# Sums by token for the convolution's norm, and half of the first residual turned ahead of the last output block

## The reference

```python
def conformer_conv(u, lw):
    a, b = jnp.split(u, 2, axis=-1)
    g = a * jax.nn.sigmoid(b)
    g = lax.conv_general_dilated(g, lw['conv_dw'][:, None, :], ...)     # 31 taps, by channel
    g = layernorm(g + lw['conv_b'], lw['conv_ln_g'], lw['conv_ln_b'])   # over the 1024 channels
    return jax.nn.silu(g) @ lw['w_conv_o']

# token_mixer:
merged = jax.nn.sigmoid(ga) * y_att + jax.nn.sigmoid(gc) * y_conv
return merged @ lw['w_out']

# first_block:
xs = xs + g1 * token_mixer(hx, lw, rope, k_c, v_c)
hx = modulate(rmsnorm(xs, norm2_g[l]), sh2, sc2)
xs = xs + g2 * peer_ffn(hx, lw)                                        # begins with hx @ peer_wq
```

## Time and profile before

| | |
|---|---|
| median of 3 runs | 2242.8 us (2241.54 to 2243.55) |
| the profiled execution | 2253.25 us, of which the span is 2251.4 us |
| TensorE busy | 95% of the span, mean granted clock 0.981 |
| VectorE, ScalarE, GpSimd busy | 76%, 42%, 41% |
| the norm (from the channel sums to the first product with `w_co`) | 468.0 to 495.5 us |
| the first residual (from the last product with `w_out` to the first with `peer_wq`) | 593.0 to 615.2 us |

### The profile page before, as it was taken

One profiled execution on the slowest core, in us unless ns is written; L12 is line 12 of the kernel. 1 busy time (PEld: TensorE's weight loads), 2 busy tenths in 40 slices (PEclk: granted clock), 3 DMA queues, 4 the chain that ended last, 5 costly groups with the idle time before them and its releaser, 6 DMA issues. The chain is left out here.

```text
span 2251.4 us, 29546 instructions
## 1 busy us (share of the span) xinstructions
PE 2136.3 (95%) x10685; PEld 1831.2 (81%) x10685; DVE 1705.4 (76%) x3336; ACT 937.5 (42%) x1480; POOL 929.4 (41%) x614
## 2 busy tenths in 40 slices
PE   6998999989799999799889999999999999999998
PEld 3886787767688999799878888888888888777767
DVE  5886989886634999999678888878888897744243
ACT  3445555443333344344333333333333343445472
POOL 0251222100453655599634454434555551542222
PEclk9999999999999999899999999999999999999999
DMA  7322021345362554455889999998999994321111
GB/s 301 103 91 78 33 94 57 126 150 196 132 198 78 168 163 156 132 202 225 297 323 368 342 356 358 363 347 318 375 349 361 359 359 158 108 84 47 48 47 47
DMA packets 177136, 455.84 MB, mean 202 GB/s; under 512 B 13792, under 2 KB 80736, under 8 KB 175328
## 3 DMA queue, kind: packets, MB, share of 16 engines
q1 hardware_dynamic: 136912, 293.57, 38.2%
q0 software_dynamic: 36864, 134.23, 15.9%
q10 hardware_dynamic: 3216, 26.15, 3.1%
HBM read 409.86 MB, written 44.04 MB: 202 GB/s over the span
## 5 line engine op out<-in xcount | busy, mean ns | idle before, releaser
L1757 POOL TENSOR_TENSOR Rl<-raw,Rh 128x1024 fp32r<-128x1024 f32 x156 | 401.5, 2580 | 846.7 <-ACT Rh L1258 846.2
L1258 ACT ACTIVATE Rh<-raw 128x1024 fp32r<-128x1024 f32 x380 | 399.9, 1056 | 340.6 <-DMA raw<-in_u 105.6
L723 PE MATMUL bank<-XAh,Rh 128*128 128x384 f32 (+1 forms) x1280 | 458.7, 358 | 9.4 <-ACT gt L1592 4.2
L725 PE MATMUL bank<-XAh,Rl 128*128 128x384 f32 (+1 forms) x1280 | 444.9, 348 | 0.0
L724 PE MATMUL bank<-XAl,Rh 128*128 128x384 f32 (+1 forms) x1280 | 444.7, 347 | 0.0
L1793 POOL DMA_INDIRECT ga<-in_v,eid x128 | 197.5, 1543 | 185.9 <-DVE y L2433 158.4
L1841 DVE TENSOR_TENSOR Rl<-raw,Rh 128x1024 fp32r<-128x1024 f32 x212 | 260.4, 1230 | 7.3 <-ACT Rh L1258 7.2
L1793 POOL DMA_INDIRECT ga<-in_un,eid x128 | 172.7, 1349 | 221.1 <-DVE act L2425 183.6
L723 PEld LDWEIGHTS bank<-XAh,Rh 128*128 128x128 f32 x1280 | 243.0, 190 | 21.2 <-issue 6.9
L724 PEld LDWEIGHTS bank<-XAl,Rh 128*128 128x128 f32 x1280 | 242.9, 190 | 10.8
L725 PEld LDWEIGHTS bank<-XAh,Rl 128*128 128x128 f32 x1280 | 242.2, 189 | 10.5
(11 more groups left out here) (335 smaller groups left out, 4019.5 us busy)
## 6 DMA issues: line engine op xcount, KB each, us to landing
raw<-in_u SPq DMA_DIRECT2D x128, 512.0 KB
raw<-in_v SPq DMA_DIRECT2D x128, 512.0 KB
wd<-wb ACTq DMA_DIRECT2D x12, 2048.0 KB, 7.2
wg<-wd SPq DMA_DIRECT2D x30, 768.0 KB
raw<-in_w_mod SPq DMA_DIRECT2D x32, 512.0 KB
raw<-in_w_in SPq DMA_DIRECT2D x32, 512.0 KB
gd<-pk SPq DMA_DIRECT2D x64, 192.0 KB, 1.9
gt<-gd SPq DMA_DIRECT2D x16, 768.0 KB, 11.3
```

The lines of the kernel that those rows point to most:

```text
L723: e.matmul(o, sh, mh, start=first, stop=False)
L725: return e.matmul(o, sl, mh, start=False, stop=last)
L1258: e.activation(Rh[:, r % NRING, :], raw[:, n % NRAW, :], ACT.Copy).then_inc(s["hi"], 1)
L1757: e.tensor_tensor(Rl[:, r % NRING, :], raw[:, n % NRAW, :], Rh[:, r % NRING, :].bitcast(F32), ALU.subtract).then_inc(s["lo"], 1)
```

## The change

**The norm.** The matrix that adds the channels up for the mean is now `mean8`, filled once with 1/1024, so that the result in PSUM is the mean, and the eight subtractions read it there. The squares are summed by token: each 128 x 128 piece of a block of squares is the stationary operand and one column of ones the moving one, so that the result is 128 tokens by 4 (column `tb`). Variance, root and reciprocal are then taken on 128 x 4 elements. Four diagonal matrices (`dgr`: the identity, each row scaled by its token's reciprocal) times the all-ones matrix spread the result over all partitions, in PSUM (`rsd`), and the eight multiplications read it there. TensorE does this ahead of ao 7. On VectorE `merge_att(5)` moves behind the norm, to 6 and 7.

**The residual.** After wo 6 TensorE turns the four halves with i = 0 (blocks 0 to 3 of `cout`), then does wo 7, and then the four with i = 1. VectorE adds the first four, with `mod_bias`, and adds an epsilon to their sums of squares, all between the evictions of wo 6 and wo 7. ScalarE squares 128 x 512 at a time. The order of the root, the reciprocal and the normed block over the four token blocks is staggered: the mean square of block b + 1 stands ahead of `h2` of block b.

```diff
+    use(("rsd",), 4, 0)
     for cb in range(8):
+        if cb == 7:
+            for tb in range(4):
+                use(("x1", tb, 0), 4 + tb)
         use(("wo", cb), cb % 4)
     for tb in range(4):
-        for i in range(2):
-            use(("x1", tb, i), 4 + (2 * tb + i) % 4)
+        use(("x1", tb, 1), 4 + tb)
...
             for cb in range(8):
                 e.wait_ge(s["conv"], cb + 1)
-                t = e.matmul(o[:, :], ones[:, :], cout[:, cb, :], start=(cb == 0), stop=(cb == 7))
+                t = e.matmul(o[:, :], mean8[:, :], cout[:, cb, :], start=(cb == 0), stop=(cb == 7))
...
                 e.wait_ge(s["sqc"], cb + 1)
-                e.matmul(o[:, :], ones[:, :], lt[cb % 4][:, :], start=(cb == 0), stop=(cb == 7)).then_inc(s["ltv"], 1)
+                for tb in range(4):
+                    t = e.matmul(o[:, tb:tb + 1], lt[cb % 4][:, tb * 128:(tb + 1) * 128], ones[:, 0:1],
+                                 start=(cb == 0 and tb == 0), stop=(cb == 7 and tb == 3))
+                t.then_inc(s["ltv"], 1)
+            o, done = hold(("rsd",))
+            e.wait_ge(s["sub"], 8)
+            for tb in range(4):
+                e.wait_ge(s["dgr"], tb + 1)
+                t = e.matmul(o[:, tb * 128:(tb + 1) * 128], ones[:, :], dgr[:, tb, :], start=True, stop=True)
+            t.then_inc(done, 1)
             merge_att(7)
...
+            def turned_out(i):
+                for tb in range(4):
+                    o, done = hold(("x1", tb, i))
+                    if tb == 0:
+                        u = USES["wo", 4 * i + 3]
+                        e.wait_ge(free[u.bank], u.done)
+                    for k in range(4):
+                        t = e.transpose(o[:, k * 128:(k + 1) * 128],
+                                        cout[:, 4 * i + k, tb * 128:(tb + 1) * 128], ident[:, :])
+                    t.then_inc(done, 1)
             for cb in range(8):
+                if cb == 7:
+                    turned_out(0)
                 gemm_T(("w_o", cb), XB, ("wo", cb), merged_ready if cb == 0 else None)
-            add_T("x1", lambda k, sl: cout[:, k, sl], y1_ready)
+            turned_out(1)
... ScalarE
-            for b in range(4):
-                u = USES["x1", b, 1]
-                e.wait_ge(free[u.bank], u.done)
-                e.activation(jk2[:, :], x1[:, b, :], ACT.Square, accum_out=sml[:, 128 + 2 * b:129 + 2 * b]
-                             ).then_inc(s["sqd"], 1)
-                root(f"h2{b}", sml[:, 129 + 2 * b:130 + 2 * b])
+            for i in range(2):
+                for b in range(4):
+                    u = USES["x1", b, i]
+                    e.wait_ge(free[u.bank], u.done)
+                    o = 104 + 4 * i + b
+                    e.activation(jk2[:, 0:512], x1[:, b, 512 * i:512 * i + 512], ACT.Square, accum_out=sml[:, o:o + 1]
+                                 ).then_inc(s["sqd"], 1)
+                    if i:
+                        root(f"h2{b}", sml[:, 112 + b:113 + b])
... VectorE
-            e.tensor_scalar(mu[:, :], bank[u.bank][:, :], 1.0 / D, None, ALU.mult).then_inc(free[u.bank], 1)
             for cb in range(8):
-                e.tensor_tensor(cout[:, cb, :], cout[:, cb, :], mu[:, :], ALU.subtract).then_inc(s["sub"], 1)
+                e.tensor_tensor(cout[:, cb, :], cout[:, cb, :], bank[u.bank][:, :], ALU.subtract).then_inc(s["sub"], 1)
...
+                if cb == 6:
+                    e.wait_ge(s["x1"], 16)
+                    added(0)
+                    t_mod = mod_bias(24, 40, 0, n_own)
+                    e.wait_ge(s["sqd"], 4)
+                    t_sq = own(e.tensor_scalar(sml[:, 104:108], sml[:, 104:108], D * EPS, None, ALU.add))
+            added(1)
```

More of the change, by code:

```diff
@@ L452, in build @@
         lu = [at(f"lu{i}", FB + 60 + 2 * i, [128, 512]) for i in range(4)]
-        mu = at("mu", FB + 64, [128, 512])
-        rsd = at("rsd", FB, [128, 512])
+        mean8 = at("mean8", 70, [128, 128])
+        dgr = at("dgr", FB, [128, 4, 128])
         x1 = at("x1", FB + 44, [128, 4, 1024])
@@ L942, in merged_ready @@
                 e.wait_ge(s["mRl"], k + 1)
+            def turned_out(i):
[4 more added lines that the diff above has]
+                        e.wait_ge(free[u.bank], u.done)
+                    e.wait_ge(s["cn"], 8)
+                    for k in range(4):
+                        t = e.transpose(o[:, k * 128:(k + 1) * 128],
+                                        cout[:, 4 * i + k, tb * 128:(tb + 1) * 128], ident[:, :])
+                    t.then_inc(done, 1)
             for cb in range(8):
+                if cb == 7:
+                    turned_out(0)
                 gemm_T(("w_o", cb), XB, ("wo", cb), merged_ready if cb == 0 else None)
[L947 to L959, removed]
-            add_T("x1", lambda k, sl: cout[:, k, sl], y1_ready)
+            turned_out(1)
             def h2_ready():
@@ L1456, in scalar_program @@
                     ahead(CH["w_ao", 7])
-            root("conv", rsd[:, :])
+            root("conv", sml[:, 56:60])
             ahead(CH["w_co", 3])
@@ L2113, in put_off @@
                     values_low(n - 1)
+            e.memset(mean8[:, :], 1.0 / D).then_inc(s["mean8"], 1)
             scores1(0)
@@ L2169, in vector_program @@
             e.wait_ge(s["ltv"], 8)
-            variance("conv", rsd[:, :], bank[u.bank][:, :], D)
+            v = sml[:, 56:60]
+            variance("conv", v, bank[u.bank][:, 0:4], D)
+            e.wait_ge(s["std"], ROOTS["conv"])
+            e.reciprocal(v, v).then_inc(free[u.bank], 1)
+            e.wait_ge(free[u.bank], u.done)
+            for tb in range(4):
+                e.tensor_scalar(dgr[:, tb, :], ident[:, :], v[:, tb:tb + 1], None, ALU.mult).then_inc(s["dgr"], 1)
             merge_att(4)
[L2172 to L2175, removed]
+            u = USES["rsd",]
+            e.wait_ge(full[u.bank], u.full)
             e.wait_ge(s["sub"], 8)
             def conv_normed(cb):
-                e.tensor_tensor(cout[:, cb, :], cout[:, cb, :], rsd[:, :], ALU.mult).then_inc(s["cn"], 1)
+                e.tensor_tensor(cout[:, cb, :], cout[:, cb, :], bank[USES["rsd",].bank][:, :], ALU.mult
+                                ).then_inc(s["cn"], 1)
             def conv_low(cb):
@@ L2198, in vector_program @@
             conv_low(7)
-            merge_att(6)
-            merge_att(7)
+            for cb in range(5, 8):
+                merge_att(cb)
             modulation(24, 26)
@@ L2220, in vector_program, with added @@
                                 ).then_inc(s["mRl"], 1)
+            def added(i):
+                for tb in range(4):
+                    u = USES["x1", tb, i]
+                    v = x1[:, tb, i * 512:(i + 1) * 512]
+                    e.wait_ge(full[u.bank], u.full)
+                    e.tensor_tensor(v, v, bank[u.bank][:, :], ALU.add).then_inc(free[u.bank], 1)
             e.wait_ge(s["cRh"], 8)
@@ L2229, in vector_program, with variance2 @@
                     modulation(34 + cb, 35 + cb)
[L2230 to L2242, removed]
-            for b in range(4):
[L2246 to L2250, removed]
+                if cb == 6:
+                    e.wait_ge(s["x1"], 16)
+                    added(0)
+                    e.wait_ge(s["wmod"], 24)
+                    t_mod = mod_bias(24, 40, 0, n_own)
+                    e.wait_ge(s["sqd"], 4)
+                    t_sq = own(e.tensor_scalar(sml[:, 104:108], sml[:, 104:108], D * EPS, None, ALU.add))
+            added(1)
+            def variance2(b):
+                e.wait_ge(s["sqd"], 5 + b)
+                e.tensor_scalar(sml[:, 112 + b:113 + b], sml[:, 104 + b:105 + b], sml[:, 108 + b:109 + b], 1.0 / D,
+                                ALU.add, ALU.mult).then_inc(s["var"], 1)
+            after(t_sq)
+            variance2(0)
+            t = invert("h20", sml[:, 112:113])
+            for b in range(4):
+                if b < 3:
+                    variance2(b + 1)
+                after(t)
+                e.tensor_scalar(h2[:, b, :], x1[:, b, :], sml[:, 112 + b:113 + b], None, ALU.mult).then_inc(s["h2s"], 1)
+                if b < 3:
+                    t = invert(f"h2{b + 1}", sml[:, 113 + b:114 + b])
             after(t_mod)
```

19 lines of the change are left out of this document (9 added, 10 removed).

## The result

The changed kernel took 2258.05 us (median of 4 executions, 2256.4 to 2260.13), the kernel before 2243.18 us beside it (4 executions, 2241.54 to 2243.57): a ratio of 1.0061, with a 95% interval of 1.0046 to 1.0075. That is 14.9 us, and outside the stated range. The profiled execution took 2257.39 us, with a span of 2255.6 us, where the profiled one of before had 2251.4. The two profiled executions are only 4.2 us apart, because that of before was itself 10 us above its median; so the timed comparisons say how much, and the traces where. One execution of a later kernel (e10) took 3576 us, at a mean granted clock of 0.556; the ratios leave it out.

What follows compares the result with a forecast made beforehand. TensorE, busy 95% of the span, was taken as the bound. VectorE's chain -0.12, transposes +1.96, earlier root -2.2 and token blocks -0.9 summed to -1.3 us: 2242.8 to 2241.5, range 2237.7 to 2244.6.

Steps and rivals of the forecast that it cites:

- Then three merges stand there instead of two: 0.60 back.: VectorE behind the convolution's last rest: one more merge costs 0.60 us of the 0.72 gained, leaving 0.12 net.
- co 0 can start when its first rest is there, 494.7: TensorE after ao 7: co 0 waits only for its first rest, so co 7 finishes about 2 us earlier.
- the squares by token: Norm, TensorE: 32 one-column matmuls, 0.5 to 0.9 us per four, done between 482 and 484, before VectorE asks at 484.5.
- The way from the variance to the first multiplication: Norm: 2.1 us from 484.5, so the blocks are multiplied from 486.6, 3.8 us earlier.
- The gain of the norm does not arrive: Convolution: silu waits for w_co 3, so it comes 0.72 us earlier, at 492.3, not 3.8 earlier.
- The 0.72 us that the earlier load was to bring: Load of w_co 3 follows VectorE's modulation 23, which moves with the subtractions, so it lands 0.72 us earlier, at 489.93.
- The rival in which it arrives (0.09): Chance 0.09: w_co 3 lands before the norm is done, silu up to 3.3 us sooner; -4.6 us in all, 2238.2.
- 16 transposes ahead of wo 7: Residual, TensorE: 16 transposes at 0.123 us with nothing to hide them make wo 7 end 1.96 us later.
- VectorE's wait for the four squares: Residual: over before wo 7's eviction, 1.4 to 2.6 us in hand; rival with squares later, chance 0.04.
- D: Start of wo 7's eviction; root forecast at D + 4.4 against D + 6.61, 2.2 us gained; token blocks gain 0.9 more.
- The clock did not fall in wo 7: Rival, chance 0.08: transposes between products lower the clock in wo 7, +1.0 to +3.5 us, 2243.8 to 2246.3.
- The table load: Residual, ScalarE: 1.28 us, ending last before the root; rival that it costs 1.3 us more, chance 0.05, 2242.8.

Runs made afterwards that it cites:

- e10: Kernel before with the residual change alone, plus ScalarE's weight conversions reordered (w_co 0 and 1 ahead of the root); 2247.97 us, 0.9995 of before.
- e5: The changed kernel, timed again beside the kernel before; 2259.69 us, 1.0055 of before.
- e8: The changed kernel with merge_att(5) put back ahead of the norm's multiplications, timed again on another chip; 2248.60 us, 1.0003 of before.
- e6: The changed kernel with merge_att(5) left late and only co 3's bank changed from 7 to 5; 2248.72 us, 1.0006 of before.
- e1: The changed kernel with merge_att(5) put back ahead of the norm's multiplications, first timing; 2250.97 us, 1.0011 of before.
- e3: Kernel before with the norm change alone, merge_att(5) in its old place, residual as before; 2249.08 us, 1.0001 of before.
- e4: Kernel before with the residual change alone, first timing; 2243.77 us, 0.9984 of before.
- e9: Kernel before with the residual change alone, timed again on another chip; 2246.81 us, 0.9996 of before.

## Why the prediction was wrong

**The step that failed** is "Then three merges stand there instead of two: 0.60 back." It priced a moved step by its own length on its own engine, and by the 0.6 us that all behind it on VectorE shift. It did not ask who waits for what the step *gives back*. A merge reads a bank and frees it. The bank's next use stands in `psum_plan`, two lines below that of ao (ao 5 and co 3 both 7), and the statement that takes four banks at once made the wait for one a wait for all. "co 0 can start when its first rest is there, 494.7" was the sentence in which it should have been seen. It cost 10.3 us at the last joined block by the trace, 9.9 to 10.9 counted from the mean, and 11.1 us of time (e5 against e8). The forecast sum had 0.60 for it.

The longer effect in time than in the trace is not wholly explained. Both traces of the changed kernel are some 8 us behind before's at the first product with `peer_wq`, counted from the mean, and the time was 12.0 and 14.9 us over; the slow products there are 1.6 of the difference. Behind `peer_wq` executions of the same kernel drift apart by several microseconds: e6's profiled one was 2.5 us ahead of before's at the first product with `peer_wq` and 11.4 ahead at the end, and its median was no faster. Whether the late start costs more in those stages was not tested.

**A term that was mis-sized: the squares by token.** The bound was 0.5 to 0.9 us for four small products, from transposes, so 3.9 to 7.4 in all. They took 10.34 us in the changed kernel, 10.33 in e8, 11.85 in e1. Two things were missed. The row says x64: each of the 32 products has two records, where a transpose has one. And the granted clock fell while they ran. The stretches of the changed kernel (busy time of TensorE, weight loads, VectorE, ScalarE, GpSimd; granted clock; share of the DMA engines; GB/s), the whole one first and then a part ahead of the fall and a part behind it:

```profile
476.00:487.00 11.00, 10.30 (x64) 10.21 (x64) 8.32 (x16) 6.39 (x11) 0.00 (x0) 0.67 0.43 139
476.00:479.00 3.00, 3.00 (x28) 3.00 (x28) 3.00 (x6) 3.00 (x6) 0.00 (x0) 1.00 0.03 5
481.00:486.00 5.00, 5.00 (x25) 5.00 (x25) 2.96 (x5) 0.94 (x1) 0.00 (x0) 0.50 0.77 243
```

and before:

```profile
476.00:485.00 9.00, 7.70 (x20) 3.77 (x21) 9.00 (x15) 6.75 (x10) 0.00 (x0) 1.00 0.24 63
```

A clock of 0.67 is a mix of the two levels, 2.4 and 1.2 GHz; before, with the wide sums, it stood at 2.4. From the start of one record to the next it is 0.11 us at 1.00 (28 records, 476.0 to 479.0) and 0.21 at 0.50 (25 records, 480.8 to 485.9). An estimate from the first: all 64 at 1.00 would have taken 7.2 us, at the upper end of the bound, and ended at 483.2, ahead of VectorE at 484.0. So it was the fall of the clock, near 479.7, that made VectorE wait 2.37 us for the sum. The sooner the clock fell, the longer the row: it fell 3.8 us into the row in the changed kernel and in e8 (10.3 us in all), 3.1 us into it in e6 (10.98) and 2.1 in e1 (11.85).

The way from the variance to the first multiplication was also longer, 3.16 us for 2.1: the last of the diagonals was ready at 487.86 and the multiplication began at 489.50, 1.64 us for the 0.4 to 0.6 of the last spreading product and its signals. So of 3.8 us by which the blocks were to be multiplied earlier, 0.3 was left (490.42 - 475.08 = 15.3 us behind the mean before, 489.50 - 474.47 = 15.0 now). This alone would have cost little: the forecast had none of that gain arrive.

**What was right**, by its own steps:

- The gain of the norm does not arrive. Silu came 18.2 us behind the mean in the changed kernel, and 17.9 before; ScalarE still stood 0.76 us for w_co. The 0.72 us that the earlier load was to bring did not come either: SyncE issued it earlier, but it landed later behind the mean (ScalarE began to convert it at 15.9 us, before at 15.6). The rival in which it arrives (0.09) did not come about: e3 is 1.0001.
- Reading PSUM costs nothing: eight subtractions 4.87 us. Diagonals 0.88 for four, 1.0 forecast.
- 16 transposes ahead of wo 7: 1.91 us; from eviction to eviction 7.20 us, where a product alone is 5.44, so 1.76 were added, for 1.96.
- VectorE's wait for the four squares ended at 601.05, and after the small addition it stood 2.45 us until the eviction: inside the 1.4 to 2.6 in hand. GpSimd's subtraction ran beside the four adds (596.54 to 598.93) and did not hold them up (2.47 us).
- Root at D + 4.28 (forecast 4.4) right behind the table load; last `h2` at D + 8.30, forecast 8.3 to 8.4, before 11.43. The residual's net at the last `h2`: 1.76 - 3.13 = -1.4 us (-1.14 forecast).
- The clock did not fall in wo 7 (1.00 from 596 to 604). The table load is 1.28 us and the root follows it within 0.02 (606.65, 607.95). It stands last in the chain now, as foreseen, so its whole price shows. The Trainium skill ("ScalarE: Activation LUTs", What ACT_TABLE_LOAD costs) gives 1.38 us of draining beside the load. The traces do not agree: here and at 492.71 behind 491.41 + 1.28, nothing stands between the load and the operation that needs it.

**The range and the chances.** The slower side held 0.05, all of it on small mechanisms. That a moved read of a bank makes a new wait was not among the rivals. Of the versions here the residual's half alone is the best supported (e4 and e9, -0.16% and -0.04%), and only e4 is clear of none. The norm's half adds nothing to it that could be measured.

## What to carry to other kernels

When a change moves an instruction that reads a buffer or a bank, look up the buffer's *next* writer and where that stands in its engine's program, before anything is said of the instruction's own cost. A wait that takes several buffers at once is as late as the latest of them. And if such a wait appears, look first whether another bank is free: one number (e6) did what moving the work (e1) did. Of a gain in the middle of a stage, ask of each engine in turn what it has queued ahead of the next step; here ScalarE had its conversions and TensorE the slowed sum, so a shorter VectorE step brought nothing. And a wait that one trace shows may be missing in the next execution of the same code.

## What the runs showed of the hardware

- An f32 product with one moving column is far from free: 32 of them took 10.3 us, 0.32 each on average (0.22 at a granted clock of 1.00, 0.43 at 0.50), more than the eight products with 512 columns that they replaced (7.11 us). Each has two records of TensorE and two of its weight load; the loads were busy as long as the products (3.00 us of 3.00), and which of the two sets the pace is not shown.
- TensorE's granted clock fell from 1.00 to 0.50 in the middle of this row, in all seven traces that have it, while TensorE was busy without a gap. In the five with the wide sums it stayed at 1.00 there. In the changed kernel it did not come back until 4.3 us into ao 7, whose first nine products took 3.99 us, 0.44 each instead of 0.23; in e1, where it had fallen 3.6 us behind the mean instead of 5.3, it was back 1.1 us into ao 7.
- The clock also rose while TensorE did nothing but transposes. In e4 they begin at 605.80 at 0.50, behind 6.40 us of standing, and from 609 on the clock is 1.00, 5 us ahead of the next product (614.40).
- A table load costs 1.28 us where nothing hides it, and nothing beside it.
